# Attention: splits of query and output weights placed elsewhere, output product begun inside the loop; the experts' gather takes x in hi and lo parts

## What is computed

```
# experts (first block): two of 32 experts for each token, rows gathered by expert
xbuf = zeros(n_rows, D).at[slot_dest].set(repeat(xf, 2))
hdn  = silu(xb @ w1[e]) * (xb @ w3[e]);  y = hdn @ w2[e]
out  = einsum('tk,tkd->td', gates, y_slots)
# window attention (second block, layer 1): 16 heads of 64, 4 key/value heads
s    = q @ k * 64**-0.5 - slope * |i - j|, NEG where |i - j| > 128
attn = exp(s - m) / (sum(exp(s - m)) + exp(sink - m))
y    = (attn @ v) @ w_out
```

## Time and profile before

| | before |
|---|---|
| median of 3 runs | 1775.91 us (1775.62 to 1776.52) |
| profiled execution, own time | 1779.97 us |
| its span | 1778.3 us |
| mean granted clock of TensorE | 0.962 |
| PE busy | 1643.8 us, 92% |
| DVE busy | 744.0 us, 42% |
| ACT busy | 468.7 us, 26% |
| POOL busy | 61.6 us, 3% |

### The profile page before, as it was taken

How to read it: one execution, slowest core, us unless ns; L and a number is a source line. 1 busy time by engine, 2 the same in 40 slices (tenths; PEclk the granted TensorE clock), 3 DMA queues, 4 the chain that set the end, 5 groups by cost and what they waited for, 6 DMA issues and landing times.

```text
span 1778.3 us, 21675 instructions
## 1 busy us (share of the span) xinstructions
PE 1643.8 (92%) x9078; PEld 1193.3 (67%) x9078; DVE 744.0 (42%) x1006; ACT 468.7 (26%) x539; POOL 61.6 (3%) x104
## 2 busy tenths in 40 slices
PE   8996899999999997999999589999999996799997
PEld 7744333333333336999884449999899985689997
DVE  1675311111111116545510745444745565655455
ACT  1340100000000003334300214344334434533342
POOL 2000000000000000000100010000000000000000
PEclk9996999999999998999999799999999998899999
DMA  6606299999999999655324127555455212258500
GB/s 199 228 14 270 109 422 422 422 422 422 422 422 422 422 408 340 207 189 189 119 95 142 48 86 270 191 187 189 166 190 185 97 49 95 95 204 294 189 24 25
DMA packets 162702, 395.23 MB, mean 222 GB/s; under 512 B 10914, under 2 KB 111392, under 8 KB 138064
## 3 DMA queue, kind: packets, MB, share of 16 engines
q1 hardware_dynamic: 159904, 385.67, 58.2%
q0 software_dynamic: 2736, 8.68, 1.4%
HBM read 393.28 MB, written 1.05 MB: 222 GB/s over the span
## 4 chain that ended last, share of the span: by engine, by line
PE 67%; DMA 15%; DVE 9%; SPq 4%; issue 3%; ACT 2%; POOL 1%; POOLq 0%; DVEq 0%; ACTq 0%
PE bank L1254 27%; DMA ring<-in_moe_w_dram 14%; PE bank L1267 11%; PE bank L837 5%; PE bank L850 4%; PE bank L1382 3%; PE bank L866 2%; PE bank L653 2%; PE bank L1367 2%; SPq L282 2%; PE bank L1455 2%; SPq L257 2%; PE bank L1242 1%; PE bank L1755 1%; PE bank L600 1%
## 5 line engine op out<-in xcount | busy, mean ns | idle before, releaser
L837 PE MATMUL bank<-ring,arena 128*64 128x512 f32 x1024 | 260.2, 605 | 24.7 <-DMA ring<-in_moe_w_dram 20.7
L837 PEld LDWEIGHTS bank<-ring,arena 128*64 128x64 f32 x1024 | 102.8, 138 | 158.3 <-issue 75.0
L1254 PE MATMUL bank<-x_hi,split_u_hi 128*128 128x256 f32 x688 | 195.0, 283 | 0.0
L1254 PE MATMUL bank<-x_hi,split_u_lo 128*128 128x256 f32 x688 | 194.7, 283 | 0.0
L1254 PE MATMUL bank<-x_lo,split_u_hi 128*128 128x256 f32 x688 | 194.7, 283 | 0.0
L1254 PE MATMUL bank<-x_lo,split_g_hi 128*128 128x256 f32 x656 | 185.6, 283 | 0.0
L1254 PE MATMUL bank<-x_hi,split_g_lo 128*128 128x256 f32 x656 | 185.6, 283 | 0.0
L1254 PE MATMUL bank<-x_hi,split_g_hi 128*128 128x256 f32 x656 | 185.6, 283 | 0.0
L1174 DVE TENSOR_TENSOR split_g_lo<-ring,split_g_hi 128x2048 fp32r<-128x2048 f32 x47 | 107.7, 2293 | 139.6 <-ACT split_g_hi L1168 139.6
L1028 DVE SCALAR_TENSOR_TENSOR arena<-arena,work 128x256 f32<-128x256 f32 x32 | 15.4, 481 | 311.5 <-PE bank L866 311.5
L1174 DVE TENSOR_TENSOR split_u_lo<-ring,split_u_hi 128x2048 fp32r<-128x2048 f32 x45 | 103.2, 2293 | 71.4 <-ACT split_u_hi L1168 71.4
(11 more groups left out here) (331 smaller groups left out, 2388.3 us busy)
## 6 DMA issues: line engine op xcount, KB each, us to landing
ring<-in_moe_w_dram SPq DMA_DIRECT2D x192, 1024.0 KB, 12.1
ring<-in_ffn_w_in_dram SPq DMA_DIRECT2D x88, 1024.0 KB, 5.2
ring<-in_ffn_w_out_dram SPq DMA_DIRECT2D x44, 1024.0 KB, 5.0
ring<-in_ml_w_in_dram SPq DMA_DIRECT2D x12, 1024.0 KB, 5.0
ring<-in_rec_w_in_dram SPq DMA_DIRECT2D x10, 1024.0 KB, 11.6
ring<-in_at_w_in_dram SPq DMA_DIRECT2D x6, 1024.0 KB, 5.0
ring<-in_rec_w_out_dram SPq DMA_DIRECT2D x5, 1024.0 KB, 13.8
gb_row<-in_ln_g_dram POOLq DMA_DIRECT2D x8, 512.0 KB, 7.3
```

The costliest lines, as they stand in the source:

```text
L837: i = nc.tensor.matmul(bank[4 + p][64 * j:64 * j + 64, :], xe[p][:, k, :], unit_view(n, 4)[:, k % 4, :], start=(k == 0), stop=(k == KT - 1))
L1254: i = nc.tensor.matmul(up_bank(kind, s_)[:, m * T:(m + 1) * T], w, xp_[b][:, k, :], start=(k == 0 and j == 0), stop=(k == KT - 1 and j == 2))
```

## The change

The gather: ACT writes the hi part of x_tok beside the transposes' copies, DVE the lo part ahead of the routing; onehot becomes fp32r, and each fp32 product becomes two fp32r ones. On DVE the diagonals come right behind onehot, then the banks' copies with a memset between, the rows' copies, the memset of h_e, and `place` last. PE makes the rows as soon as banks 0 and 1 are copied, and waits for their copies only in the first `combine`, for the memset only in the first `turn`. The attention: splits 4 and 5 stand ahead of the first queries' copies and pair 0's weights, split 6 where they stood, 7, 8 and 9 in rounds 0, 2 and 4 ahead of `mixed`; the output product begins in rounds 5 and 6, and (1, 0) without its last chunk follows the last mix.

```diff
@@ -115,6 +115,8 @@
                       for i, part in enumerate(("hi", "lo"))]
+        xt_hi, xt_lo = [nc.alloc_sbuf_tensor_at(f"xt_{part}", [P, TT, D], F32R, offset=parts_at + i * TT * D * 4)
+                        for i, part in enumerate(("hi", "lo"))]
         h_hi = sb("h_hi", [P, 2, 2, T], F32R)
@@ -190,10 +192,10 @@
         mo = {n: sem("moe_" + n) for n in (
-            "logit", "e1", "e2", "exp1", "exp2", "assign", "rank", "pos", "gath", "gath_ev", "start", "xe",
+            "logit", "xt_hi", "xt_lo", "pos1", "gath_a", "e1", "e2", "exp1", "exp2", "assign", "rank", "pos", "gath", "gath_ev", "start", "xe",
             "ha", "hb", "silu", "h", "tr", "hT", "y", "ysb", "h0", "diag", "rows", "rows_sb", "sel", "comb")}
         xs = arena[:, 0:KT * 768].rearrange("p (k s) -> p k s", k=KT)
-        onehot = arena[:, 6144:7168].rearrange("p (t s) -> p t s", t=TT)
+        onehot = nc.alloc_sbuf_tensor_at("onehot", [P, TT, SLOTS], F32R, offset=arena_at + 6144 * 4)
         xe = [arena[:, 7168 + i * 512:7680 + i * 512].rearrange("p (k c) -> p k c", k=KT) for i in range(2)]
@@ -555,6 +557,10 @@
                 for b in range(2):
+                    if L == 0:
+                        act.wait_ge(G["ln_half"], 2 * t + b + 1)
+                        h = slice(b * HALF, (b + 1) * HALF)
+                        nc.scalar.activation(xt_hi[:, t, h], x_tok[:, t, h], ACT.Copy).then_inc(mo["xt_hi"], 1)
                     act.wait_ge(G["ln_tr"], 4 * L + 2 * t + b + 1)
@@ -812,19 +818,22 @@
             pe.wait_ge(mo["pos"], 1)
+            pe.wait_ge(mo["xt_lo"], 2 * TT)
             for k in range(KT):
                 for t in range(TT):
-                    i = nc.tensor.matmul(bank[k][:], x_tok[:, t, k::KT], onehot[:, t, :],
-                                         start=(t == 0), stop=(t == TT - 1))
+                    for n, part in enumerate((xt_hi, xt_lo)):
+                        i = nc.tensor.matmul(bank[k][:], part[:, t, k::KT], onehot[:, t, :],
+                                             start=(t == 0 and n == 0), stop=(t == TT - 1 and n == 1))
                 i.then_inc(mo["gath"], 1)
-            pe.wait_ge(mo["gath_ev"], KT)
+            pe.wait_ge(mo["gath_a"], 1)
+            pe.wait_ge(mo["gath_ev"], 1)
             pe.wait_ge(mo["diag"], 1)
             i.then_inc(mo["rows"], 1)
-            pe.wait_ge(mo["rows_sb"], 2)
-            pe.wait_ge(mo["h0"], 1)
+            pe.wait_ge(mo["gath_a"], KT // 2)
+            pe.wait_ge(mo["gath_ev"], KT // 2)
@@ -852,6 +861,8 @@
             def turn(e, p):
+                if isinstance(e, int) and e == 0:
+                    pe.wait_ge(mo["h0"], 1)
                 pe.wait_ge(mo["h"], e + 1)
@@ -859,6 +870,8 @@
+                if first:
+                    pe.wait_ge(mo["rows_sb"], 2)
                 pe.wait_ge(mo["ysb"], e + 1)
@@ -922,6 +935,12 @@
             th = own.then
+            for t in range(TT):
+                for b in range(2):
+                    h = slice(b * HALF, (b + 1) * HALF)
+                    dve.wait_ge(mo["xt_hi"], 2 * t + b + 1)
+                    nc.vector.tensor_tensor(xt_lo[:, t, h], x_tok[:, t, h], xt_hi[:, t, h].bitcast(F32), ALU.subtract) \
+                        .then_inc(mo["xt_lo"], 1)
             dve.wait_ge(mo["logit"], 1)
@@ -993,20 +1012,27 @@
                 th(nc.vector.tensor_scalar(onehot[:, t, :], iota_s[:], v_pos[0][:, t:t + 1], None, ALU.is_equal))
-                i = nc.vector.scalar_tensor_tensor(out=onehot[:, t, :], in0=iota_s[:], scalar=v_pos[1][:, t:t + 1],
-                                                   in1=onehot[:, t, :], op0=ALU.is_equal, op1=ALU.add)
-            i.then_inc(mo["pos"], 1)
-            own.did(nc.vector.memset(xs[:, :, SLOTS:], 0.0))
-            for k in range(1, KT, 2):
+                nc.vector.scalar_tensor_tensor(out=onehot[:, t, :], in0=iota_s[:], scalar=v_pos[1][:, t:t + 1],
+                                               in1=onehot[:, t, :].bitcast(F32), op0=ALU.is_equal, op1=ALU.add) \
+                    .then_inc(mo["pos" if t == TT - 1 else "pos1"], 1)
+
+            def gathered(k):
                 dve.wait_ge(mo["gath"], k + 1)
                 nc.vector.tensor_copy(xs[:, k, 0:SLOTS], bank[k][:]).then_inc(mo["gath_ev"], 1)
-
             i.then_inc(mo["diag"], 1)
-
+            gathered(1)
+            own.did(nc.vector.memset(xs[:, :, SLOTS:], 0.0))
+            for k in range(3, KT, 2):
+                gathered(k)
+            dve.wait_ge(mo["rows"], 1)
+            for j in range(2):
+                nc.vector.tensor_copy(rows_b[:, 2 * j:2 * j + 2, :], bank[j][:].rearrange("p (v t) -> p v t", v=2)) \
+                    .then_inc(mo["rows_sb"], 1)
+            nc.vector.memset(h_e[0:64, :], 0.0).then_inc(mo["h0"], 1)
             for b in range(BLOCKS):
@@ -1014,12 +1040,6 @@
                 th(nc.vector.tensor_scalar(place[:, b, :], place[:, b, :], -1.0, None, ALU.add))
-            dve.wait_ge(mo["rows"], 1)
-            for j in range(2):
-                nc.vector.tensor_copy(rows_b[:, 2 * j:2 * j + 2, :], bank[j][:].rearrange("p (v t) -> p v t", v=2)) \
-                    .then_inc(mo["rows_sb"], 1)
-
-            nc.vector.memset(h_e[0:64, :], 0.0).then_inc(mo["h0"], 1)
             dve.wait_ge(mo["rows_sb"], 2)
@@ -1074,7 +1094,7 @@
                 act.wait_ge(mo["gath"], k + 1)
-                nc.scalar.activation(xs[:, k, 0:SLOTS], bank[k][:], ACT.Copy).then_inc(mo["gath_ev"], 1)
+                nc.scalar.activation(xs[:, k, 0:SLOTS], bank[k][:], ACT.Copy).then_inc(mo["gath_a"], 1)
@@ -1110,7 +1130,8 @@
             pool.wait_ge(mo["start"], 1)
-            pool.wait_ge(mo["gath_ev"], KT)
+            pool.wait_ge(mo["gath_a"], KT // 2)
+            pool.wait_ge(mo["gath_ev"], KT // 2)
@@ -1768,16 +1789,23 @@
                     queries(i + 3)
-                if i == PAIRS - 1:
+                if i == 5:
+                    pe.wait_ge(at["wlo"], 8)
+                    pe.wait_ge(at["ylo"], 4)
+                    project(0, 0, range(0, 4))
+                if i == 6:
+                    project(0, 1, range(0, 4))
+                if i == 7:
                     pe.wait_ge(at["wlo"], 10)
-                    pe.wait_ge(at["ylo"], PAIRS - 1)
-                    project(0, 0, range(KT - 1))
+                    pe.wait_ge(at["ylo"], 7)
+                    project(0, 0, range(4, 7))
+                    project(0, 1, range(4, 7))
                 mix(i)
-            project(0, 1, range(KT - 1))
+            project(1, 0, range(KT - 1))
             pe.wait_ge(at["ylo"], PAIRS)
-            project(0, 0, (KT - 1,))
-            project(0, 1, (KT - 1,))
-            project(1, 0, range(KT))
+            for hf in range(2):
+                project(0, hf, (KT - 1,))
+            project(1, 0, (KT - 1,))
             project(1, 1, range(KT))
@@ -1786,6 +1814,8 @@
                 nc.scalar.activation(ka_T[:, g, :], bank[g][:, 0:T], ACT.Copy).then_inc(at["ka"], 1)
+            for n in (4, 5):
+                at_split_act(act, n)
@@ -1818,8 +1848,7 @@
             exps(0)
-            for n in (4, 5):
-                at_split_act(act, n)
+            at_split_act(act, 6)
             exps(1)
@@ -1827,15 +1856,17 @@
                     exps(i + 2)
+                if i in (0, 2, 4):
+                    at_split_act(act, 7 + i // 2)
                 mixed(i)
-                if i < 4:
-                    at_split_act(act, 6 + i)
             nc.vector.tensor_copy(va_t, bank[2][:].rearrange("p (t d) -> p t d", t=TT)).then_inc(at["va"], 1)
+            for n in (4, 5):
+                at_split_dve(dve, n)
@@ -1874,18 +1905,17 @@
             weights(0)
-            for n in (4, 5):
-                at_split_dve(dve, n)
             weights(1)
+            at_split_dve(dve, 6)
             normalise(0)
                     normalise(i + 1)
+                if i in (0, 2, 4):
+                    at_split_dve(dve, 7 + i // 2)
                 mixed(i)
-                if i < 4:
-                    at_split_dve(dve, 6 + i)
```

## The result

The changed kernel takes 1753.05 us (median of 4 runs, 1751.96 to 1755.53) where the one before took 1776.19 beside it (1775.62 to 1776.52): ratio 0.9872, 95% interval 0.9858 to 0.9887, 23.1 us faster. Forecast were 1752.5 and 23.4.

The account below looks back on a forecast made before the run. Bounds: before the experts' DMA-bound loop, when its transfers can start; in the attention, the ACT and DVE chain. Gather 14.0 plus attention 9.4 gave 23.4, from 1775.91 to 1752.5 us; range 1748.5 to 1760.

Parts of the forecast that it names:

- Gather end: Experts' gather: 32 fp32r records, eight cold, 24 at 0.228 us with strided loads hidden, end 6.7 us earlier.
- After the gather: Gather end to expert 0: rows' product right behind the gather, place operations later; expert 0 starts another 5.65 us earlier.
- Warm expert 0: Expert 0 to its silu: without a long PE gap before it, runs at 2.4 GHz, saving 1.7 us.
- Gather stage: Experts' routing and gather up to expert 0's silu: 14.0 us saved, all carried through the DMA-bound loop.
- First transpose: Attention before the loop: one split instead of two ahead of it, first transpose 5.1 us earlier.
- Rounds: Attention loop, first to last transpose: 55.8 us against 55.2, a loss of 0.6, with three split rounds of 9.8.
- The second and third rival: Attention: second, it gives nothing, 1761.9 us, chance 0.07; third, clock never rises, 1779.9 us, chance 0.03.
- Tail: Attention's output product and norm: 24 products moved into rounds save 5.5 us; the norm ends late by 0.6.
- Attention: Whole attention stage: 5.1 - 0.6 + 5.5 - 0.6, 9.4 us saved; ends 5.5 and some 12.
- The strided load that sets the pace: First rival, gather: strided weight loads set the record pace; 1754.5 us at 0.313, 1760.4 in full series; chance 0.15.
- the attention that gives nothing: Second rival, attention: split ahead of y's low part makes the loop return the start's gain; 1761.9 us; chance 0.07.
- the clock that never rises: Third rival, attention: after new PE gaps everything until the output product ends runs at 1.2 GHz; 1779.9 us; chance 0.03.

Follow-up runs that it names:

- e4: Changed kernel with the gather taking 128 contiguous columns of x per bank instead of every eighth (features in another order); 1753.7 us, one run.
- e5: Changed kernel with the gather's product back in fp32, without x's hi and lo parts; new order and attention kept; 1759.54 us, ratio 0.9897.
- e6: Kernel before with only the gather's fp32r product and x's hi and lo parts; old order and attention; 1770.14 us, ratio 0.9954.
- e1: Changed kernel with the attention's edits undone, so the gather's part alone; 1762.04 us, ratio 0.9921.
- e10: Changed kernel plus unread products on the identity in PE's waits in the attention, to keep the clock up; 1753.08 us, ratio 0.9866.
- e9: Against e8, ACT's three splits inside the loop stand behind its copy of y instead of ahead of it; 1739.84 us, ratio 0.9792.
- e12: e9 plus unread identity products sized to the waits: 17 ahead of the gather, 7 ahead of pair 0's transposes; 1735.13 us, ratio 0.9758.
- e2: Kernel before with the attention's part of the change alone; 1766.41 us, ratio 0.9940.
- e7: Kernel before with only splits 4 and 5 moved ahead of pair 0's scores, nothing in their old place; 1765.41 us, ratio 0.9931.
- e8: Changed kernel with each of DVE's splits one place behind ACT's, ACT's last split moved to round 3; 1743.22 us, ratio 0.9805.
- e3: Changed kernel with the whole output product behind the attention loop, none in rounds 5 and 6; 1756.64 us, ratio 0.9883.
- e11: e9 plus unread identity products in the routing, 40 ahead of the ranks and 36 ahead of the gather; 1743.65 us, ratio 0.9813.

## Why the prediction was right

The time (1752.5 against 1753.05) came out of the right mechanisms, with sizes off that cancelled: the gather's end was put 0.7 too high, the rounds 1.4, the cost of x's parts (0.4) at nothing, and the tail 1.8 too low. That the total is met within 0.6 us is luck; the prediction's own span was 1749 to 1757.

- **Gather end, 6.7.** 5.98 (15.60 to 9.62). Eight cold records and then warm ones, as put; 0.245 a record instead of 0.228, for the strided load shows by 0.017 (e4). Taking the load as hidden was nearly right, though the strided fp32r load was 332 ns, longer than the 313 of its nearest row. (The whole sum with a load of 0.313 would have been 21.4, not the 21.3 given.)
- **After the gather, 5.65.** 5.47 (8.14 to 2.67). The one-hot of 0 holds: it took 0.49 and 0.75 with fp32r output, as before. ACT still idled 0.55 ahead of the last evacuation of the norm, so its copies fit, and DVE's subtractions were done 6.5 us before the logits; yet every kernel with them begins the work on the ranks 0.37 later (section on arithmetic or order), which the sum had at nothing.
- **Warm expert 0, 1.7.** 1.67. It comes with the order alone (7.12 in e5) and not with the shorter gather (10.12 in e6).
- **Gather stage, 14.0.** 13.1 to the silu, of which 12.8 arrive at the stage's end, the gather starting 0.4 later in the stage; 14.0 by e1's ratio. The cover of the selections was 2.26 us; the prediction's own numbers gave at least 0.25 (193.05 less 192.8).
- **First transpose, 5.1.** 5.2, once the 1.4 of clock at the stage's head is taken off (44.35 to 37.79). 
- **Rounds, minus 0.6.** Minus 2.0 (55.2 to 57.3). This is the step that failed most: two short rounds of 5.9 were 7.5 each, since every split round leaves PE a gap behind which it opens at 1.2 GHz (e10: 5.92 with the clock held). The split rounds were 9.5, not 9.8, and the first 7.4, not 8.2. The last was met, 6.38 for 6.4, by luck: I had added 2.7 for twelve products to 3.7, but at the high clock the same round takes 4.79 (e9, e10, e12), and the other 1.6 is the low clock (0.73 over that round after the change). The second and third rival both spoke of cold stretches; this was a small part of either, and I had priced them only as whole cases.
- **Tail, 5.5 less 0.6.** 6.7 net (26.20 to 19.47). 4.9 were forecast. The product starts at the high clock (1.00 in its first 5 us, 0.57 before the change), which I had taken as low; of the norm's 0.6 some 0.4 is there.
- **Attention, 9.4.** 9.9 by stages, 10.7 by e2's ratio.

**Rivals.** The strided load that sets the pace is refuted by e4 and by the pace itself; the attention that gives nothing by e2; the clock that never rises by the windows (0.99 from 1490 to 1503) and by the time. In part it came true: the low clock is back behind every round with a split (0.59 from 1486 to 1490), and rises again each time. What no rival of mine said, and e7 and e8 show: the attention's gain was only half of what the same move can give. I had written that DVE follows ACT in each split, and booked both durations as fixed; that the second can be put where it waits for nothing was in the same rows.

## What to carry to other kernels

Work that passes through two engines in a row costs both durations on a chain that alternates between them; put the second engine's part one place later, and its wait disappears (9.5-us rounds became 7.5, and 6.0 to 6.8 once ACT's copy stood ahead of its own split). Test a moved edit also with nothing in its old place: here one move of five carried the stage's gain, and the others cancelled. Products that only keep TensorE active can pay when they are shorter than the wait they fill, and cost their excess when they aren't (1739.84 without, 1735.13 with 17 in the routing and 7 in the attention, 1743.65 with 76 in the routing), so their duration has to be read from a trace first.

## What the runs showed of the hardware that I had not expected

- A strided load of the weights, 332 ns against 188 for the contiguous one, stands almost whole beside a product of 512 columns in fp32r (0.245 us a record against 0.228), though a load takes longer than the 0.228 from one record to the next.
- The clock's rise in the gather came about 3.5 us after its first record in the kernel after, and later in others with the same gather: it lasted 9.36 to 9.62 us in five profiles (after, e1, e3, e6, e10), and 10.71 and 10.77 in two (e8, e9); in e8 the windows still show 0.50 when the gather has run for 5.5 us. That phase alone is over 1 us of the kernel, as is that of the attention's head (18.64 or 17.26) and of the last feed-forward stage (194.4 or 195.9 from the last residual of norm 6 to that of norm 7).
- The fp32 products on the identity (128 columns, two records each) took 0.20 us at a granted clock of 1.00 (21 records in 2.00 us, e11) and 0.33 at 0.59 (18 in 3.00, e12). A record of 128 columns is thus 0.1 us, not a quarter of the 0.228 to 0.245 of 512 columns, so a filler's length can't be taken from its columns; its loads are 0.19 us each.
